# Where squares, roots, weights and modulation steps stand in a two-block transformer kernel on one core

## The reference

```
# first block, after the mixer
groups = rms_norm(groups, g_out.reshape(N_GROUPS, HEAD_DIM)).reshape(b, s, MIX_WIDTH)
x = x + groups @ w_out
h2 = rms_norm(x, g_ffn)
x = x + (silu(h2 @ w_gate) * (h2 @ w_up)) @ w_down
# second block
mod = (silu(c) @ w_mod + b_mod)[:, None, :]
sh1, sc1, g1, sh2, sc2, g2 = jnp.split(mod, 6, axis=-1)
h = _rms(x, norm1_w) * (1 + sc1) + sh1
...
x = x + g1 * (mixed @ w_out)
h2 = _rms(x, norm2_w) * (1 + sc2) + sh2
x = x + g2 * _conv_ffn(h2, w_up, conv_w, conv_b, w_down)
```

## Time and profile before

| | |
|---|---|
| three runs, us | 1416.92, 1418.18 (median), 1420.22 |
| the profiled execution, us | 1418.51 |
| its span, us | 1416.60 |
| mean granted clock of TensorE | 0.944 |
| TensorE matmul busy | 1289.3 us, 91% of the span |
| VectorE, ScalarE, GpSimd busy | 804.6, 514.8, 137.1 us |

### The profile page before, as it was taken

The page is one execution under the profiler, slowest core; times in us unless marked ns, Lnnn a source line. Parts: engine busy times, 40 slices in busy tenths (PEclk is TensorE's granted clock), DMA queues, the critical chain, the costliest instruction groups (busy, mean ns, idle before and its releaser), DMA issues. The chain is left out here.

```text
span 1416.6 us, 15641 instructions
## 1 busy us (share of the span) xinstructions
PE 1289.3 (91%) x6274; PEld 990.7 (70%) x6274; DVE 804.6 (57%) x1299; ACT 514.8 (36%) x817; POOL 137.1 (10%) x129
## 2 busy tenths in 40 slices
PE   6999997879999899999998975678979999999999
PEld 5786564538788678888876762346758887888877
DVE  5557664134655844656547956754875553355632
ACT  5345456544322211222224532346343441244321
POOL 0000000013200700000014700001510000000000
PEclk9999998979999989999998986589999999999999
DMA  8311112012344345444442510010212212322232
GB/s 347 106 53 38 60 61 90 1 60 80 131 168 147 106 151 205 157 156 138 149 149 67 125 31 0 1 61 30 90 46 103 90 62 102 119 89 90 71 101 82
DMA packets 24328, 138.44 MB, mean 98 GB/s; under 512 B 2973, under 2 KB 4189, under 8 KB 14912
## 3 DMA queue, kind: packets, MB, share of 16 engines
q1 hardware_dynamic: 23488, 135.81, 27.7%
q0 software_dynamic: 768, 1.63, 1.0%
HBM read 133.75 MB, written 3.67 MB: 97 GB/s over the span
## 5 line engine op out<-in xcount | busy, mean ns | idle before, releaser
L121 ACT ACTIVATE w_hi_part<-w_raw 128x2048 fp32r<-128x2048 f32 (+1 forms) x101 | 175.3, 1735 | 308.4 <-PE bank L135 296.0
L133 PE MATMUL bank<-xhi_ffn,w_hi_part 128*128 128x512 f32 x704 | 280.2, 398 | 6.6 <-DVE xlo_ffn L235 6.6
L135 PE MATMUL bank<-xhi_ffn,w_lo_part 128*128 128x512 f32 x704 | 278.5, 396 | 0.0
L134 PE MATMUL bank<-xlo_ffn,w_hi_part 128*128 128x512 f32 x704 | 278.3, 395 | 0.0
L127 DVE TENSOR_TENSOR w_lo_part<-w_raw,w_hi_part 128x2048 fp32r<-128x2048 f32 (+1 forms) x101 | 212.4, 2103 | 106.5 <-ACT w_hi_part L121 103.2
L133 PEld LDWEIGHTS bank<-xhi_ffn,w_hi_part 128*128 128x128 f32 x704 | 132.7, 188 | 38.7 <-issue 7.6
L135 PEld LDWEIGHTS bank<-xhi_ffn,w_lo_part 128*128 128x128 f32 x704 | 132.6, 188 | 31.9
L134 PEld LDWEIGHTS bank<-xlo_ffn,w_hi_part 128*128 128x128 f32 x704 | 132.8, 189 | 31.2 <-issue 0.2
L356 DVE SCALAR_TENSOR_TENSOR squares<-bank,param,squares 128x511 f32<-128x511 f32 x88 | 63.9, 747 | 91.3 <-ACT squares L339 89.8
L133 PE MATMUL bank<-hhi_half,w_hi_part 128*128 128x512 f32 x240 | 96.8, 404 | 6.5 <-DVE hlo_half L331 6.5
L133 PE MATMUL bank<-hhi,w_hi_part 128*128 128x512 f32 x240 | 95.9, 400 | 1.3 <-DVE hlo L364 1.3
(11 more groups left out here) (338 smaller groups left out, 2092.8 us busy)
## 6 DMA issues: line engine op xcount, KB each, us to landing
mod_w<-in_w_mod SPq DMA_DIRECT2D x32, 768.0 KB, 4.4
w_raw<-in_w_gu SPq DMA_DIRECT2D x22, 1024.0 KB, 4.8
w_raw<-in_w_down SPq DMA_DIRECT2D x32, 704.0 KB, 4.1
w_raw<-in_w_up SPq DMA_DIRECT2D x22, 1024.0 KB, 4.8
w_raw<-in_w_in_f SPq DMA_DIRECT2D x9, 1024.0 KB, 5.2
w_raw<-in_w_out SPq DMA_DIRECT2D x8, 1024.0 KB, 4.7
w_raw<-in_w_in SPq DMA_DIRECT2D x5, 1024.0 KB, 4.8
x<-in_x SPq DMA_DIRECT2D x4, 512.0 KB, 8.6
```

What stands on the lines that cost most here:

```text
L121: act.activation(k.whi[:, slot, 0:width], k.raw[:, slot, 0:width], ACT.Copy).then_inc(k.w_hi, 1)
L133: pe.matmul(out, whi, xhi, start=first, stop=False)
L134: pe.matmul(out, whi, xlo, start=False, stop=False)
L135: return pe.matmul(out, wlo, xhi, start=False, stop=last)
```

## The change

In the group norm ScalarE squares tiles 0 to 3 and VectorE tiles 4 to 7, each in two slots, with a semaphore of its own; TensorE takes them in the order 0, 4, 1, 5, 2, 6, 3, 7. A Sqrt of one column stands ahead, and Silu and Exp go behind the rounding. In an up tile that is the last of its half, both groups of modulation steps go behind the residue of the product. At the end of the first feed-forward a Sqrt of one column is made ahead of the second half's first down tile, and the root and its reciprocal go ahead of the last chunk's rounding and residue. In the last block GpSimd no longer adds tiles 4 and 5; TensorE sums tiles 4 to 7 by themselves.

```diff
@@ dve_up
         self.dve_weights(dve, n + 2)
-        between()
+        last = i % HALF == HALF - 1
+        if not last:
+            between()
         dve.wait_ge(self.silued, i + 1)
         dve.wait_ge(self.freed, i + 1)
         dve.tensor_tensor(up, up, gate, ALU.mult).then_inc(self.made, 1)
-        between()
+        if not last:
+            between()
         dve.wait_ge(self.rounded, i + 1)
         dve.tensor_tensor(self.hlo[:, i % HALF, :], up, self.hhi[:, i % HALF, :].bitcast(F),
                           ALU.subtract).then_inc(self.split, 1)
+        if last:
+            between()
+            between()
...
@@ ScalarE, group norm
-                modulation.start(act)
-                act.activation(col(DT), pr("log_dt"), ACT.Exp).then_inc(col_exp, 1)
-                for j in range(8):
-                    if j >= 4:
-                        act.wait_ge(gn_took, j - 3)
-                    act.activation(k.sq[:, j % 4, :], o_all[:, j, :], ACT.Square).then_inc(gn_sq, 1)
+                act.activation(sqrt_first[:, 0:1], eps_col[:, 0:1], ACT.Sqrt)
+                for j in range(4):
+                    if j >= 2:
+                        act.wait_ge(gn_took, 2 * j - 3)
+                    act.activation(k.sq[:, j % 2, :], o_all[:, j, :], ACT.Square).then_inc(gn_sq, 1)
                 act.wait_ge(gn_took, 8)
...
                     act.activation(ghi[:, j, :], o_all[:, j, :], ACT.Copy).then_inc(gn_hi, 1)
+
+                modulation.start(act)
+                act.activation(col(DT), pr("log_dt"), ACT.Exp).then_inc(col_exp, 1)
...
@@ ScalarE, down tiles
                         if half == 1:
+                            if j == 0:
+                                act.activation(sqrt_first[:, 1:2], eps_col[:, 0:1], ACT.Sqrt)
                             act.wait_ge(ffn.added, KT + j + 1)
                             r3.act_square(act, k, x[:, j, :], j)
-                        ffn.act_weights(act, ffn.down_chunk(half, j) + 2)
+                        if half == 0 or j < KT - 1:
+                            ffn.act_weights(act, ffn.down_chunk(half, j) + 2)
                 r3.act_root(act, KT, eps_col[:, 0:1])
+                ffn.act_weights(act, ffn.down_chunk(1, KT - 1) + 2)
@@ VectorE
+                for j in range(4, 8):
+                    if j >= 6:
+                        dve.wait_ge(gn_took, 2 * j - 10)
+                    dve.tensor_tensor(k.sq[:, 2 + j % 2, :], o_all[:, j, :], o_all[:, j, :], ALU.mult).then_inc(gn_sq_v, 1)
                 dve.wait_ge(gn_root, 1)
...
                         ffn.dve_down(dve, x, half, j)
-                        ffn.dve_weights(dve, ffn.down_chunk(half, j) + 2)
+                        if half == 0 or j < KT - 1:
+                            ffn.dve_weights(dve, ffn.down_chunk(half, j) + 2)
...
                 r3.dve_invert(dve)
+                ffn.dve_weights(dve, ffn.down_chunk(1, KT - 1) + 2)
@@ TensorE
-                for j in range(8):
+                for j in range(4):
                     pe.wait_ge(gn_sq, j + 1)
-                    group_sums(pe, k.bank[0], j, 8, k.sq[:, j % 4, :]).then_inc(gn_took, 1)
+                    group_sums(pe, k.bank[0], j, 8, k.sq[:, j % 2, :]).then_inc(gn_took, 1)
+                    pe.wait_ge(gn_sq_v, j + 1)
+                    group_sums(pe, k.bank[0], 4 + j, 8, k.sq[:, 2 + j % 2, :]).then_inc(gn_took, 1)
...
@@ last block, GpSimd
                 for j in (6, 7):
                     add_attn(j)
-                for j in (4, 5):
-                    r6.add(pool, k, j)
@@ last block, TensorE
-                r6.pe_sum(pe, k, KT - 3, [KT - 2, KT - 1])
+                r6.pe_sum(pe, k, KT - 5, list(range(KT - 4, KT)))
```

More of the change, by code:

```diff
@@ L626, in program @@
         eps_col = sb("eps_col", [P, 1])
+        sqrt_first = sb("sqrt_first", [P, 2])
         mods = sb("mods", [P, 48])
@@ L1415, in program @@
         ffn = FeedForward(k, "ffn", GU, io["w_gu"], io["w_down"], xhi, xlo, hhi, hlo, following=2)
-        gn_sq, gn_took, gn_root, gn_inv, gn_wide, gn_scaled, gn_hi, gn_lo, added1 = (
-            k.sem(f"group_{w}") for w in ("squared", "taken", "rooted", "inverted", "spread", "scaled",
+        gn_sq, gn_sq_v, gn_took, gn_root, gn_inv, gn_wide, gn_scaled, gn_hi, gn_lo, added1 = (
+            k.sem(f"group_{w}") for w in ("squared", "squared_v", "taken", "rooted", "inverted", "spread", "scaled",
                                           "rounded", "split", "added"))
```

## The result

| | before | after |
|---|---|---|
| median, us | 1418.06 (1416.92 to 1420.81, 6 runs) | 1395.54 (1393.51 to 1401.66, 6 runs) |
| the profiled execution, its span, us | 1418.51, 1416.60 | 1394.14, 1392.3 |
| mean granted clock | 0.944 | 0.952 |

The ratio is 0.9844, interval 0.9822 to 0.9867: 22.5 us less, where 9.5 were forecast. The first question is whether the forecast steps are there.

What follows compares the result with a forecast made beforehand. TensorE is busy nearly everywhere, so only shortening its waits or lifting its clock pays. Terms -8.5 - 0.1 + 0.1 + 0.6 - 1.6 = -9.5 took 1418.51 to 1409.0, less 0.33: 1408.7 us; range 1405.3 to 1412.8.

Steps and rivals of the forecast that it cites:

- Part A: End of the first half's up projection: TensorE's 6.5 us wait falls to 1.3 at full clock; 8.5 us gained.
- the third chunk: Rival: the up projection's wait comes back at the third chunk of down weights; 1416 to 1420 us, chance 0.03.
- Part B: Group norm: first sum 1.52 us earlier, but sums set the pace, so the root starts 0.1 us late.
- rival of the full clock: Rival: TensorE keeps its full clock through the group norm, root 2.7 us early; 1405.9 us, chance 0.10.
- rival of program order: Rival: group norm sums go in program order, eight taking 11.4 us; 1410.5 to 1412.9, given 1411.5 us, chance 0.12.
- Part C: End of the first feed-forward: root and reciprocal go ahead of the last weights; costs 0.6 us.
- Part D: Ahead of the second feed-forward: two additions go from GpSimd to TensorE, root earlier; 1.6 us gained.
- the clock behind A: Rival: the clock still falls behind the shortened wait ending the first half's up projection; 3.3 us lost, 1412.0, chance 0.12.
- the attention's clock: Rival: the clock falls throughout the second block's attention, 18 us lost; 1427 us, chance 0.03.

Runs made afterwards that it cites:

- pad32: The kernel before with one unused two-column tile behind eps_col, moving every later tile 32 bytes; 1408.55 us, ratio 0.9930.
- part_a: The kernel before with only the reordered last up tile of a half, all tiles at their old addresses; ratio 0.9929, -10.1 us.
- part_b: The kernel before with only the group norm's edit, all tiles at their old addresses; ratio 0.9989, -1.6 us.
- part_c: The kernel before with only the early Sqrt table and reordered weights ending the first feed-forward, tiles at old addresses; ratio 1.0005, +0.7 us.
- part_d: The kernel before with only the last block's edit (GpSimd's two additions gone), all tiles at old addresses; ratio 0.9987, -1.8 us.
- after_align128: The changed kernel with every tile started at a multiple of 128 bytes; 1407.69 us, ratio 0.9911 to the kernel before.

## Why the prediction was wrong, point by point

**The step that failed is a term that the sum put at nothing without a reason: the pace of the matmuls in all stretches where TensorE neither waits nor lacks its clock.** The change was read as a list of instructions that move, and each was costed. Of the early Sqrt the prediction asked only whether its pass is hidden ("at no cost"), and not what its new tile does to the tiles behind it. In its place pad32 showed that the shift of 32 bytes alone is worth 10.5 us, more than the whole forecast of 9.5: the pace of the last feed-forward fell from 233.3 to 226.8 ns. The rivals had no such case either: all of them were waits, orders and clocks at the places that the diff touches. The first sentence of the argument, that an edit pays only where TensorE waits or where its clock rises, is what shut it out. In the middle of the last feed-forward TensorE waits for nothing and has its full clock, and it still made 443 matmuls in place of 430.

**Part A, right.** A wait of 1.3 us and the full clock behind it were forecast, for 8.5; the wait was 0.5, because the residue took 1.00 and not 1.74. In part_a's trace, where the wait is 0.6, the whole first feed-forward takes 376.7 us in place of 386.0, so 9.3 less; by its runs part_a measured 10.1, with an interval that holds 8.6. The wait did not come back at the third chunk.

**Part B, right in its mechanism, its clock open.** The first sum came 1.53 earlier relative to the block (2.07 behind the table load, 3.60 before), against 1.52. The sums of 7.95 at half clock with a rise on the way were 7.04 in part_b: the root was 0.0 early, against 0.1 late. The rival of the full clock, given 0.10, is what four of six traces show: root 2.5 early against 2.7. The forecast took the clock of the one trace at hand; over the new wait it held more often than it fell. But the clock then fell behind the root, and of the 2.5 us 1.8 were left at the start of the first feed-forward (351.80 - 285.39, against 355.60 - 287.38). The rival of program order fell: eight sums in 4.60 us at full clock, where twelve steps of 0.43 and a last of 0.53 would be 5.7. In part_b they took 7.04, of which some 5.9 went at the half clock; program order's 11.4 would have become 5.9 + 5.5/2 = 8.7.

**Part C, right.** 0.6 forecast, 0.55 by the trace, +0.7 by part_c, whose interval holds nothing as well.

**Part D, right, its reason incomplete.** 1.6 forecast, 1.4 in part_d's trace, 1.8 by the runs. The root came 2.14 behind the last addition to x, where 1.9 was forecast: the prediction put only the last square's own two passes behind it, but as that square ends (1035.21 in part_d's trace) the second pass of the square before has just started (1035.20), and the last two start 0.4 later. Nor was it seen ahead that the clock would hold wherever the two sums stand in TensorE's wait, as it did in all six traces with part D and in four of the twelve without.

The sum of the parts as the runs show it, 12.3 to 12.8, would have been 1406, inside the range; with the shift it is 1395.5, 10 us below its end. The rivals on the other side (the clock behind A, the attention's clock) did not come: the grant from 828 to 968 was 0.72, with 91.5 us of matmuls, against 0.70 and 88.8.

## What to carry to other kernels

Read the allocations of a diff as you read its instructions: a tile of 8 bytes moved a whole kernel's operands and gave it 0.7%. Where TensorE is busy throughout, count the matmuls in equal windows of the two traces, before looking for waits. Then place the operands on purpose: here, all tiles alike by 256 bytes gave 1.2% to the kernel before, and made the changed kernel 1388 us in place of 1395.5, without one instruction changed.

## What the runs showed of the hardware that was not expected

- The pace of matmuls of 128 x 128 by 512 columns, each behind a load of its weights, at full clock, depends on where the moving and the stationary operand start, by their distance modulo 256 bytes: 226.8 ns at 0, 228.9 to 230.1 at 64, 232.4 to 233.0 at 128, 233.3 at 32 to either side, 233.4 at 96 and 234.3 at -96. It is the same beside idle engines as beside busy ones (233.3 both ways in before).
- The granted clock held in one execution and fell in another over the same wait with the same work around it: 2.96 us ahead of the group sums (held in four traces, the changed kernel's among them, fallen in part_b's and after_align128's), and 3.3 to 3.4 ahead of the last norm's sums (2.85, 4.4 or 5.5 us for the same six passes). A step that rests on it needs both values.
